# Attention on one core: the blocks of weights times values dealt out unevenly over the 17 steps of a head

## The reference

```python
s = einsum(q, k) * scale - slope * |t - s|      # for two maps of 64 columns each
p = softmax(s)
pd = p[:, :, 0] - lam * p[:, :, 1]              # 2048 x 2048 for the prompt, 256 x 256 for the sample
o = einsum(pd, v)                               # 128 values a head
```

## Time and profile before

| | us |
|---|---|
| median of 3 runs | 3022.05 (3017.98 to 3025.7) |
| profiled execution, its time | 3023.28 |
| its span, first to last instruction | 3021.5 |
| attention within the span | about 812 to 2105 |
| one head, step 0 to step 0 (the fourth) | 1294.28 to 1451.24 |

### The profile page before, as it was taken

How to read it: one execution, slowest core, us unless ns; L and a number is a source line. 1 busy time by engine, 2 the same in 40 slices (tenths; PEclk the granted TensorE clock), 3 DMA queues, 4 the chain that set the end, 5 groups by cost and what they waited for, 6 DMA issues and landing times. The chain is left out here.

```text
span 3021.5 us, 44677 instructions
## 1 busy us (share of the span) xinstructions
PE 2846.3 (94%) x15098; PEld 2498.6 (83%) x15098; DVE 1836.8 (61%) x2402; ACT 1734.3 (57%) x3126; POOL 1637.9 (54%) x1060
## 2 busy tenths in 40 slices
PE   3999999999899999999999999998899899899899
PEld 3899999999878788878787878886688899887687
DVE  7668766865477776767776777776886200341322
ACT  4667776776477777767777777775443321222321
POOL 5888764654266565656565666565664221130642
PEclk8999999999999999999999999999999999999899
DMA  2655464367344414131322232121664522565752
GB/s 84 194 162 175 146 178 138 120 177 202 103 116 150 107 33 102 36 97 46 77 66 71 64 79 64 36 90 40 215 209 148 206 89 76 150 177 181 264 182 104
DMA packets 281846, 374.32 MB, mean 124 GB/s; under 512 B 22923, under 2 KB 258507, under 8 KB 276140
## 3 DMA queue, kind: packets, MB, share of 16 engines
q1 hardware_dynamic: 279404, 369.14, 40.2%
q10 hardware_dynamic: 2080, 2.10, 0.2%
q0 software_dynamic: 128, 0.13, 0.0%
HBM read 258.04 MB, written 125.97 MB: 127 GB/s over the span
## 5 line engine op out<-in xcount | busy, mean ns | idle before, releaser
L1272 DVE TENSOR_REDUCE pa_half_max<-pa_score 128x1 f32<-128x1024 f32 x512 | 625.9, 1223 | 334.9 <-PE pa_score L1056 333.9
L1206 ACT ACTIVATE pa_p<-pa_score,pa_neg_max 128x1024 f32<-128x1024 f32 x512 | 567.9, 1111 | 71.4 <-DVE pa_neg_max L1278 71.3
L206 PE MATMUL ia_acc<-ia_xh,ia_wh 128*128 128x384 f32 x1344 | 461.9, 344 | 76.1 <-DVE ia_xl L686 43.4
L1117 PE MATMUL pa_o_acc<-pa_wt,pa_vv 128*128 128x256 f32 x2048 | 512.7, 381 | 1.8 <-ACT pa_o_out_s L1241 1.6
L1052 PE MATMUL pa_score<-pa_ka,pa_qa 128*128 128x512 f32 x1024 | 456.0, 445 | 19.3 <-ACT pa_p L1206 8.1
L1184 ACT ACTIVATE pa_wt<-pa_turned 128x512 f32<-128x512 f32 x512 | 306.5, 599 | 270.7 <-PE pa_turned L1086 269.2
L207 PE MATMUL ia_acc<-ia_xl,ia_wh 128*128 128x384 f32 x1344 | 458.1, 341 | 0.0
L208 PE MATMUL ia_acc<-ia_xh,ia_wl 128*128 128x384 f32 x1344 | 457.9, 341 | 0.0
L443 POOL TENSOR_TENSOR ia_w_sums<-ia_raw 128x512 f32<-128x512 f32 x240 | 334.6, 1402 | 177.8 <-PE ia_acc L208 159.8
L1056 PE MATMUL pa_score<-pa_kb,pa_qb 96*128 96x512 f32 x1024 | 422.9, 413 | 0.0
L1117 PEld LDWEIGHTS pa_o_acc<-pa_wt,pa_vv 128*128 128x128 f32 x2048 | 367.4, 191 | 47.5 <-ACT pa_o_out_s L1241 2.7
(11 more groups left out here) (284 smaller groups left out, 5340.1 us busy)
## 6 DMA issues: line engine op xcount, KB each, us to landing
ia_raw<-attn_w_in SPq DMA_DIRECT2D x46, 1024.0 KB, 6.7
qk_hi<-ia_hi SPq DMA_DIRECT2D x96, 192.0 KB, 3.1
qk_lo<-ia_c SPq DMA_DIRECT2D x96, 192.0 KB, 2.9
pa_ka<-qk_hi SPq DMA_DIRECT2D x32, 512.0 KB, 6.4
fl_slices<-normed SPq DMA_DIRECT2D x26, 512.0 KB, 6.5
ia_h<-x_cols SPq DMA_DIRECT2D x24, 384.0 KB, 6.3
v<-ia_c SPq DMA_DIRECT2D x48, 192.0 KB, 6.1
attn_gate<-ia_c SPq DMA_DIRECT2D x48, 192.0 KB, 1.9
```

Source lines behind the costliest of these rows:

```text
L206: pe.matmul(out, a_hi(k), b_hi(k), start=first and n == 0, stop=False)
L1117: mm = pe.matmul(o_acc[:], vv[:, k], wt[:, g % 2, k], start=k == 0, stop=k == NB - 1)
L1206: act.activation(dst[:, half * HALF:(half + 1) * HALF], score[:, (4 * q + j) % RING].rearrange("p a b -> p (a b)"), ACT.Exp, bias=neg_max[ ...
L1272: dve.tensor_reduce(half_max[:, q % 2, n, half:half + 1], score[:, (4 * q + j) % RING].rearrange("p a b -> p (a b)"), AX_X, ALU.max).then_ ...
```

## The change

The 130 blocks of a head become one stream in the order of the pairs, and a table says how many of them each quarter of each step computes. The counts by step are 7, 7, 8, 7, 8, 7, 8, 8, 8, 8, 8, 7, 11 in steps 4 to 16, and 8, 8, 6, 6 in steps 0 to 3 of the next head. The order of S, T, P and V is the same. Pairs now end within a step: after P0 of steps 6, 8 and 1, after P1 of steps 10, 12, 14, 16 and 3; the sample still ends with a step, step 3. ScalarE copies an output at a new place, after take 0 (for P0) or after exp 0 (for P1), and only the sample's at the start of the next step. SyncE stores it one step later than before. TensorE waits for the turned weights four times a pair, once for each four blocks, where it waited once or twice.

```diff
-        def product_at(q):
-            if q == 0:
-                return NP - 2, 1, 1
-            if q in (1, 2):
-                return NP - 1, q - 1, 1
-            if q == 3:
-                return NP, 0, 1
-            return (q - 4) // 2, q % 2, 0
-
-        OUT_AT = {1: (NP - 2, 1), 3: (NP - 1, 1), 4: (NP, 1), **{2 * g + 6: (g, 0) for g in range(NP - 2)}}
+        QUARTERS = {4: (2, 2, 2, 1), 5: (2, 2, 2, 1), 6: (2, 2, 2, 2), 7: (2, 2, 2, 1), 8: (3, 2, 2, 1), 9: (2, 2, 2, 1),
+                    10: (2, 2, 2, 2), 11: (2, 2, 2, 2), 12: (2, 2, 2, 2), 13: (2, 2, 2, 2), 14: (2, 2, 2, 2), 15: (2, 2, 2, 1),
+                    16: (3, 2, 3, 3), 0: (2, 2, 2, 2), 1: (2, 2, 2, 2), 2: (2, 2, 1, 1), 3: (2, 2, 1, 1)}
+        stream = [(g, k) for g in range(NP) for k in range(NB)] + [(NP, 0), (NP, 1)]
...
+                        copied_at[(q, x) if x < 3 else (q + 1, None)] = g, back
+                        out_of.setdefault((q + 1) % STEPS, []).append((g, 1 if (q + 1) % STEPS <= 4 else 0))
...
                 def pair_product(h, q, quarter):
+                    for g, k, back in products_of[q][quarter]:
+                        acc = o_acc[:]
+                        if k == 0:
                             wait(pe, o_copied, OUTS * (h - back) + g)
+                        if g == NP:
+                            if k == 0:
+                                pe.wait_ge(turned_out, unit(h, 1, "w", 0) + 1)
+                            mm = pe.matmul(acc, vv[:, NB + k], wt_s[:, k], start=k == 0, stop=k == 1)
+                        else:
+                            if k % 4 == 0:
+                                t, kind, c = last_turn(g, k // 4)
+                                late = back and 2 * g + 3 < STEPS
+                                pe.wait_ge(turned_out, unit(h, t, kind, c) + 1 - (UNITS if late else 0))
+                            mm = pe.matmul(acc, vv[:, k], wt[:, g % 2, k], start=k == 0, stop=k == NB - 1)
+                        if k == (1 if g == NP else NB - 1):
                             mm.then_inc(pair_done, 1)
...
+                    copy_out(None)
                     take(0)
+                    copy_out(0)
                     take(1)
                     exp(0)
+                    copy_out(1)
                     take(2)
```

More of the change, by code:

```diff
@@ L896, in turned_block, with last_turn @@
             return (t - 2) % STEPS
-        def product_at(q):
-            if q == 0:
-                return NP - 2, 1, 1
-            if q in (1, 2):
-                return NP - 1, q - 1, 1
-            if q == 3:
-                return NP, 0, 1
-            return (q - 4) // 2, q % 2, 0
-        OUT_AT = {1: (NP - 2, 1), 3: (NP - 1, 1), 4: (NP, 1), **{2 * g + 6: (g, 0) for g in range(NP - 2)}}
+        QUARTERS = {4: (2, 2, 2, 1), 5: (2, 2, 2, 1), 6: (2, 2, 2, 2), 7: (2, 2, 2, 1), 8: (3, 2, 2, 1), 9: (2, 2, 2, 1),
+                    10: (2, 2, 2, 2), 11: (2, 2, 2, 2), 12: (2, 2, 2, 2), 13: (2, 2, 2, 2), 14: (2, 2, 2, 2), 15: (2, 2, 2, 1),
+                    16: (3, 2, 3, 3), 0: (2, 2, 2, 2), 1: (2, 2, 2, 2), 2: (2, 2, 1, 1), 3: (2, 2, 1, 1)}
+        BLOCKS = {q: sum(sizes) for q, sizes in QUARTERS.items()}
+        stream = [(g, k) for g in range(NP) for k in range(NB)] + [(NP, 0), (NP, 1)]
+        products_of, out_of, copied_at, begun = {}, {}, {}, 0
+        for q, n in BLOCKS.items():
+            taken = [(g, k, 1 if q < 4 else 0) for g, k in stream[begun:begun + n]]
+            begun += n
+            sizes = QUARTERS[q]
+            assert sum(sizes) == n
+            products_of[q] = [taken[sum(sizes[:x]):sum(sizes[:x + 1])] for x in range(4)]
+            for x, part in enumerate(products_of[q]):
+                for g, k, back in part:
+                    if k == (1 if g == NP else NB - 1):
+                        assert (g, k, back) == part[-1] and x != 2
+                        copied_at[(q, x) if x < 3 else (q + 1, None)] = g, back
+                        out_of.setdefault((q + 1) % STEPS, []).append((g, 1 if (q + 1) % STEPS <= 4 else 0))
+        assert begun == len(stream)
+        def last_turn(g, c):
+            turn = ((2 * g + 3) % STEPS, "w", c)
+            return max(turn, (1 + c, "v", c), key=lambda x: place[x]) if g == 0 else turn
         def is_first(h):
@@ L924, in step_parts @@
                         pairs=not (first and q < 4) and (scored or q < 4),
-                        out=q in OUT_AT and not (first and q < 6) and (scored or q < 5))
+                        out=q in out_of and not (first and q < 6) and (scored or q < 5))
         def run(eng, step):
@@ L990, in step @@
                         load_q(h, nxt) if nxt < NP else load_q(h + 1, 0)
-                    if parts["out"]:
-                        g, back = OUT_AT[q]
+                    for g, back in out_of[q] if parts["out"] else ():
                         hold(sp, sp_held, o_copied, OUTS * (h - back) + g + 1)
@@ L1098, in pair_product @@
                 def pair_product(h, q, quarter):
[L1099 to L1103, removed]
+                    for g, k, back in products_of[q][quarter]:
+                        acc = o_acc[:]
+                        if k == 0:
                             wait(pe, o_copied, OUTS * (h - back) + g)
-                            for k in range(2):
-                                mm = pe.matmul(o_acc[:], vv[:, NB + k], wt_s[:, k], start=k == 0, stop=k == 1)
-                            mm.then_inc(pair_done, 1)
[L1108 to L1119, removed]
+                        if g == NP:
[8 more added lines that the diff above has]
+                            mm = pe.matmul(acc, vv[:, k], wt[:, g % 2, k], start=k == 0, stop=k == NB - 1)
+                        if k == (1 if g == NP else NB - 1):
+                            mm.then_inc(pair_done, 1)
                 def sum_squares(n):
@@ L1232, in exp, with copy_out @@
                             exponential_sample(h, j)
-                    if parts["out"]:
-                        g, back = OUT_AT[q]
+                    def copy_out(x):
+                        if (q, x) not in copied_at:
+                            return
+                        g, back = copied_at[(q, x)]
+                        if is_first(h) and back or is_past(h) and not back:
+                            return
                         act.wait_ge(pair_done, OUTS * (h - back) + g + 1)
```

## The result

The median went from 3020.82 us (14 runs, 3011.91 to 3025.70) to 3026.49 us (14 runs, 3022.07 to 3035.26): 5.7 us or 0.19% slower, where 4.5 was forecast. The ratio over all the runs, which goes by more than the middle one, is 1.0027, 95% interval 1.0017 to 1.0038, or some 8 us (5 to 11). Either is within the 0.3% that counts here as no change, and the interval excludes a gain. The likeliest case of the prediction is the one that came.

A forecast was written before the change was run, and what follows sets the result against it. TensorE was taken to bound attention, with only its stalls to win; +0.39 us a head gave 2.7 over seven heads, plus 0.5 in head 0 and 1.3 after head 7: +4.5, a median of 3027 us, range 3012 to 3040.

The forecast's parts named there:

- Wait A: S1 waits for exp 2 of the step before; steps 7 to 10 together +0.04 us, the sample's S1 +0.43.
- Wait B: V waits for take 3; fewer blocks ahead gain nothing; step 2 -0.43, step 3 +0.85, step 5 -0.43 us.
- Step 4's copy: P0 of step 4 waited 0.21 us for the sample's copy; a longer step 3 ends this; step 4 -0.98.
- Step 16: Eight to eleven blocks, S1's stall and the moved copy: +1.77 us a head.
- wait C: T3 of step 16 waits for take 2, standing 0.75 us; blocks behind T3 fill nothing, the copy adds +0.28.
- Added waits and in-step copies at 0: 23 further waits a head for turned weights and copies within steps outside step 16 were put at 0.
- After head 7: Two more blocks, +0.86 us, and an exposed copy between the sixth and seventh pair, +0.4; total +1.3.
- Rival 1: Thinned steps keep their block as S1's stall falls away: -1.3 to -0.9 us a head, 3016; chance 0.12.
- 2 (the stalls fill): TensorE's stalls really fill, also before V and T3: half of 34 us won, 3005; chance 0.08.
- 3: Each of 23 further waits a head costs 0.06 us: 11 in all, 3038; chance 0.14.
- 4: Copies at pair ends show: 36 us, 3063, or at the lower price 6 to 8, 3034; chance 0.10.
- 5, a clock that falls: Clock falls once a head where T3 of step 16 stands 1.2 us: 13 us, 3040; chance 0.04.

The follow-up runs named there:

- a_restored: Changed kernel with steps 7, 8 and 9 back at four quarters of two blocks and step 16 at 3, 2, 2, 2; one time, 3020.65 us.
- b_block_before_v: Changed kernel with one block of step 2 moved from behind V to ahead of it; single time 3028.49 us.
- copy16_late: Changed kernel with ScalarE's copy of the finished output in step 16 moved behind take 2; one time, 3035.04 us.
- six_and_order: Six blocks in steps 2, 3, 4, none behind V, eight elsewhere; P2 ahead of T3 in step 16 and S3 in step 1; 3007.39 us, ratio 0.9947.
- ac_restored: Changed kernel with steps 7, 8, 9, 15 and 16 back at four quarters of two blocks; 3013.90 us, ratio 0.9976.
- waits_each: Changed kernel with a wait for turned weights ahead of every block of the pairs instead of every fourth; 3029.87 us, ratio 1.0024.
- looped twin of the last kernel: Six blocks in steps 2, 3, 4, P2 ahead of T3 in step 16, heads looped: 3007.21 us; the last kernel writes heads 1 to 6 out: 2985.97 us.

## Why the prediction was right

Point by point, by its steps:

- **TensorE bounds, and only its stalls can be won.** Right. Blocks were moved and none removed; the time followed the stalls. One premise is loosely told: V stands in steps 1 to 5, and step 5's is half a unit (two transposes, 0.22), which is how its 9.45 and step 1's 8.35 come out.
- **Wait A** (+0.04 for steps 7 to 10, and the 0.43 of the sample's S1). Right in kind: S1 starts 0.05 behind exp 2, and a_restored took the stall away. Its term was too small: steps 7 to 10 gained 0.24 instead of 0.04 (37.17 for 36.93). The working priced the lateness of S1 alone, which it had right at 0.30; the matmul behind a stall takes up to 0.1 more (T0 of step 10 starts 2.56 into the step for 2.16), and so steps 8, 9 and 10 are 0.04, 0.07 and 0.10 longer than forecast.
- **Wait B** (steps 2, 3 and 5). Right: -0.49, +0.82 and -0.45 in the fourth head against -0.43, +0.85 and -0.43, and b_block_before_v got the block back by moving it ahead of V.
- **Step 4's copy.** Right: P0 no longer waits, -0.94 against -0.98.
- **Step 16,** +1.77. Exactly that: S1 0.43 later, T0 to T1 0.20 longer (a block less the copy's 0.23), T1 to T3 0.28 longer, and 0.86 behind T3. Three of its parts were tried: the copy on wait C 0.27 for 0.28 (copy16_late), the blocks behind T3 (a_restored), wait C itself (six_and_order). One part was only half understood: the 0.23 saved where P0 had waited for a copy is owed to where the pair ends; a pair that ends in P0 pays 0.20 of it back in P1 (ac_restored).
- **Added waits and in-step copies at 0.** Right for the waits (waits_each) and for the copies of steps 6 to 14, which kept their 9.2.
- **Head 0** +0.52: measured 0.7, step 11 left out.
- **After head 7** +1.3: measured 1.1, with the clock's 1.68 taken out.
- **The sum.** +4.5 forecast; 5.9 by the steps, 5.46 between the medians without the loop, 5.7 with it. The 0.2 a head that the steps have above the forecast is wait A's term. How near the medians come is in part luck, since by the ratio of all runs it is some 8. The loop's late starts were 4.3 us in the profiled execution before and 5.6 after; they vary between executions of the kernels here, and can't be put down to the deal.
- **The rivals.** Rival 1 (the thinned steps keep their block) and 2 (the stalls fill) fall with the steps of after; 3 with waits_each; 4 showed in no step but 16; 5, a clock that falls, did come, but at the loop's ends in looped kernels, after head 7 and, with or without the change, in the first steps of head 0; within heads 1 to 7 it never did for a stall of a step, though T3 stood 1.0 us there.

What stayed open: why the loop's end costs more in some kernels and executions (1.96 to 3.70 us late), what TensorE waits for there, and why the stage before attention gains when the heads are written out.

## What to carry to other kernels

Before work is levelled over steps, ask of each stall which wait ends it and what lies ahead of that wait in the engine's order. Work placed ahead fills the stall, work behind it is paid in full, and a step made shorter can only be as short as the chain through the other engines: here the same 130 blocks cost 157.5, 157.0 or 155.2 us by their place. And where a loop's end idles TensorE for some microseconds, look at the clock of the first step behind it.

## What the runs showed of the hardware

Two things were not expected. A loop over two heads cost 12 us of attention in the looped twin of the last kernel: first scores 3.1 to 3.7 us late at two of three ends, and then half clock for part of a step, 1.5 us each. In the kernel before it cost 6 (1291.7 for 1285.8, on two chips). The Trainium skill (TensorE: Matmul & The Clock Gate, HAM oscillation — how this bites in real kernels) tells of such half-clock starts behind idle stretches; the trace agrees, with 0.50 in the window behind 3.35 us of idle and 1.00 in the heads, where stalls of 1.0 us left it alone. But length of idle alone does not sort the late starts here: behind 2.06 us in ac_restored the clock fell (step 0 of 10.76), behind 2.61 us in the changed kernel it did not (9.12). And a stall costs TensorE more than its idle: the distance to the second matmul was 0.34 us instead of 0.24.
